# One-hot rows for eight tokens a step in two buffers, and coefficient blocks taken in pairs

## The reference

```python
    s1, i1 = lax.top_k(sc[:, :, 0], PEER_TOPK)
    s2, i2 = lax.top_k(sc[:, :, 1], PEER_TOPK)
    cand = (s1[..., :, None] + s2[..., None, :]).reshape(n_tok, PEER_HEADS, PEER_TOPK * PEER_TOPK)
    ...
    gate = jax.nn.softmax(top_s, axis=-1).astype(xn.dtype)
    ...
        hid = jax.nn.gelu(jnp.einsum('td,thkd->thk', tc, u[ec]), approximate=False)
        return jnp.einsum('thk,thkd->td', gc * hid, v[ec])
```

## Time and profile before

| | |
|---|---|
| median of 3 runs | 2471.43 us (2470.43 to 2473.3) |
| the profiled execution's own time | 2470.42 us |
| its span, first to last instruction | 2468.6 us |
| PE busy | 2433.4 us (99%) |
| DVE busy | 1891.4 us (77%) |
| ACT busy | 1256.3 us (51%) |
| granted PE clock | 1.00 |

### The profile page before, as it was taken

The page is one execution under the profiler, slowest core; times in us unless marked ns, Lnnn a source line. Parts: engine busy times, 40 slices in busy tenths (PEclk is TensorE's granted clock), DMA queues, the critical chain, the costliest instruction groups (busy, mean ns, idle before and its releaser), DMA issues.

```text
span 2468.6 us, 48181 instructions
## 1 busy us (share of the span) xinstructions
PE 2433.4 (99%) x17669; PEld 2253.8 (91%) x17669; DVE 1891.4 (77%) x3674; ACT 1256.3 (51%) x2092; POOL 132.4 (5%) x115
## 2 busy tenths in 40 slices
PE   9999999999999999999999999999999999999999
PEld 8999998999999888999988999999889999899999
DVE  6789997666666788889996666666887767887774
ACT  6755884444444434455874444444335445656343
POOL 0042000000000000052000000000000001100000
PEclk9999999999999999999999999999999999999999
DMA  7445677666665555546677666655554555634555
GB/s 241 143 158 184 191 204 249 207 214 213 210 200 188 188 187 171 189 146 201 188 219 236 213 210 207 213 196 188 187 187 144 174 183 182 142 103 156 182 182 165
DMA packets 191991, 465.16 MB, mean 188 GB/s; under 512 B 81530, under 2 KB 83706, under 8 KB 190944
## 3 DMA queue, kind: packets, MB, share of 16 engines
q1 hardware_dynamic: 118592, 419.47, 52.5%
q0 software_dynamic: 6624, 24.28, 3.3%
q10 hardware_dynamic: 66624, 19.40, 3.2%
HBM read 442.50 MB, written 20.59 MB: 188 GB/s over the span
## 4 chain that ended last, share of the span: by engine, by line
PE 49%; DVE 2%; ACT 1%; issue 0%; DMA 0%; DVEq 0%; ACTq 0%
PE acc L896 14%; PE work L550 9%; PE work L552 9%; PE work L551 9%; PE acc L550 2%; PE acc L551 1%; PE acc L552 1%; PE work L910 1%; PE work L1126 1%; DVE ring_lo L544 1%; PE work L1112 0%; PE work L1099 0%; DMA ring<-in_u 0%; ACT ring_hi L538 0%; PE work L1100 0%
## 5 line engine op out<-in xcount | busy, mean ns | idle before, releaser
L544 DVE TENSOR_TENSOR ring_lo<-ring,ring_hi 128x1024 fp32r<-128x1024 f32 (+1 forms) x757 | 918.8, 1217 | 421.0 <-ACT ring_hi L538 419.3
L538 ACT ACTIVATE ring_hi<-ring 128x1024 fp32r<-128x1024 f32 (+1 forms) x797 | 832.3, 1051 | 440.6 <-PE acc L896 359.8
L550 PE MATMUL work<-normed_hi,ring_hi 128*128 128x256 f32 (+1 forms) x2544 | 722.3, 284 | 10.2 <-DVE ring_lo L544 5.9
L551 PE MATMUL work<-normed_lo,ring_hi 128*128 128x256 f32 (+1 forms) x2544 | 713.3, 280 | 0.0
L552 PE MATMUL work<-normed_hi,ring_lo 128*128 128x256 f32 (+1 forms) x2544 | 713.3, 280 | 0.0
L896 PE MATMUL acc<-ring_hi,weighed 128*128 128x512 f32 x2048 | 587.3, 396 | 3.0 <-DVE weighed L2033 3.0
L550 PEld LDWEIGHTS work<-normed_hi,ring_hi 128*128 128x128 f32 x2544 | 478.7, 188 | 23.2 <-DVE ring_lo L544 7.1
L551 PEld LDWEIGHTS work<-normed_lo,ring_hi 128*128 128x128 f32 x2544 | 478.1, 188 | 8.3
L552 PEld LDWEIGHTS work<-normed_hi,ring_lo 128*128 128x128 f32 x2544 | 478.0, 188 | 0.0
L896 PEld LDWEIGHTS acc<-ring_hi,weighed 128*128 128x128 f32 x2048 | 372.2, 188 | 82.6 <-issue 3.2
L550 PE MATMUL work<-arena_parts,ring_hi 128*128 128x256 f32 (+1 forms) x1184 | 336.0, 284 | 2.8 <-DVE arena L2292 2.1
(11 more groups left out here) (304 smaller groups left out, 2411.2 us busy)
## 6 DMA issues: line engine op xcount, KB each, us to landing
ring<-in_u SPq DMA_DIRECT2D x256, 512.0 KB, 3.9
ring<-in_v SPq DMA_DIRECT2D x256, 512.0 KB, 4.2
ring<-in_ffn_in SPq DMA_DIRECT2D x88, 512.0 KB, 3.7
ring<-in_query SPq DMA_DIRECT2D x32, 512.0 KB, 3.8
ficients_of_later_chunks<-gate_b ACTq DMA_DIRECT2D x32, 512.0 KB, 4.9
arena<-ficients_of_later_chunks POOLq DMA_DIRECT2D x32, 512.0 KB, 4.0
ring<-in_ffn_out SPq DMA_DIRECT2D x32, 512.0 KB, 4.0
ring<-in_even_in SPq DMA_DIRECT2D x27, 512.0 KB, 4.5
```

Source lines behind the costliest of these rows:

```text
L538: act.activation(ring_hi[:, n % RING, 0:width], ring[:, n % RING, 0:width], ACT.Copy).then_inc(hi_ready, 1)
L544: eng.tensor_tensor(ring_lo[:, n % RING, 0:width], ring[:, n % RING, 0:width], ring_hi[:, n % RING, 0:width].bitcast(F32), ALU.subtract).t ...
L550: pe.matmul(out, w_hi, hi, start=start, stop=False, **more)
L551: pe.matmul(out, w_hi, lo, start=False, stop=False, **more)
```

## The change

Rows are made for eight tokens at a time (`GROUP`, a group g of two blocks; 32 groups a stage). There are two buffers of `hot_second` and of `hot_gated`, one for even and one for odd g, and two of `first`, the second one in the space of two hidden chunks that are not written until late in the stage. The instructions of DVE for 16 tokens are then seven in place of twelve: F (first), S (second), L (low part of the gated rows, all eight tokens) and H (high part of the second four tokens) for an even g, F, S and G (both parts) for an odd g. ACT still makes the high part of the first four tokens of an even g. DVE's wait for PE now stands ahead of S, for the last block of group g - 2. PE takes two blocks behind each other after every sixth step, and the last two blocks singly. ACT's list is in another order. The buffers are laid out anew in the same space.

```diff
@@ buffers @@
-        hot_first = sb("hot_first", [P, 3, 2, NKEYS, 2], F16)
...
+        pieces = desk[:, :].bitcast(F16).rearrange("p (n x) -> p n x", x=GROUP * NKEYS)
+        last_held = arena[:, (HELD - 2) * S:HELD * S].bitcast(F16)
+        hot_second = [pieces[:, n, :].rearrange("p (a e t) -> p a e t", e=NKEYS, t=2) for n in (0, 3)]
+        hot_gated = [pieces[:, n:n + 2, :].rearrange("p x (a e t) -> p x a e t", e=NKEYS, t=2) for n in (1, 4)]
+        hot_first = [v.rearrange("p (a e t) -> p a e t", e=NKEYS, t=2) for v in (pieces[:, 6, :], last_held)]
@@ PE @@
-                def coefficients(w, count):
+                def coefficients(w, c):
...
-                    b = count % 4
+                    g, b = c // 2, c // 2 % 2
...
-                    pe.wait_ge(hots_ready, count + 1)
-                    if b == 0:
-                        pe.wait_ge(act_gated, count // 4 + 1)
+                    pe.wait_ge(hots_ready, l * GROUPS + g + 1)
+                    if c % 4 == 0:
+                        pe.wait_ge(act_gated, (l * S // BLOCK + c) // 4 + 1)
...
-                            if q % 3 == 2:
+                            if q % 6 == 5 and q < K * BESIDE - 1:
+                                for c in (q // 3 - 1, q // 3):
+                                    coefficients(w0 + c, c // 4 * 4 + ORDER[c % 4])
+                            elif q >= K * BESIDE - 4 and q % 3 == 2:
                                 c = q // 3
-                                coefficients(w0 + c, built + c // 4 * 4 + ORDER[c % 4])
+                                coefficients(w0 + c, c // 4 * 4 + ORDER[c % 4])
@@ ACT @@
                 def gelu_beside(u):
                     act.wait_ge(beside_done, l * BESIDE + u + 1)
+                    if SEGMENTS[1][2] + u == HELD - 2:
+                        act.wait_ge(hots_ready, (l + 1) * GROUPS - 2)
...
                 def gate_rows(j):
                     act.wait_ge(gates_ready, l + 1)
-                    act.wait_ge(hots_used, l * (S // BLOCK) + 4 * j + 1)
+                    act.wait_ge(hots_used, l * GROUPS + 2 * j + 1)
                     if j:
-                        act.wait_ge(*done(W0[f"expert{l}.1"] + 4 * (j - 1) + ORDER.index(0)))
+                        act.wait_ge(*done(W0[f"expert{l}.1"] + 2 * (2 * j - 2) + 1))
...
-                            gate_rows(2 * p)
+                            if p == 0:
+                                gate_rows(0)
                             split_hi(act, n)
                             store(c)
                             store(c + 1)
                             gelu_beside(u)
                             store(c + 2)
+                            gate_rows(2 * p + 1)
+                            store(c + 3)
                             split_hi(act, n + 1)
-                            store(c + 3)
-                            gate_rows(2 * p + 1)
+                            gelu_beside(u + 1)
                             store(c + 4)
-                            gelu_beside(u + 1)
                             store(c + 5)
                             split_hi(act, n + 2)
-                            store(c + 6)
-                            gelu_beside(u + 2)
-                            store(c + 7)
+                            if p < PAIRS - 1:
+                                gelu_beside(u + 2)
+                                store(c + 6)
+                                gate_rows(2 * p + 2)
+                                store(c + 7)
+                            else:
+                                store(c + 6)
+                                gelu_beside(u + 2)
+                                store(c + 7)
@@ DVE @@
+                def one_hots(g, w):
...
+                    count, b, tok, final = l * GROUPS + g, g % 2, g * GROUP, g == GROUPS - 1
+                    first = hot_first[0 if final else g % 2]
+                    if g % 2 == 0 and count or final:
+                        dve.wait_ge(act_gated, (count + 1) // 2)
+                    if count >= 2:
+                        dve.wait_ge(hots_ready, count if final else count - 1)
+                    shape = [P, 4, P, 2]
...
                     dve.tensor_tensor(first, keys, row(0), ALU.is_equal).then_inc(hots_used, 1)
+                    if g >= 2:
+                        dve.wait_ge(*done(w + 2 * (g - 2) + 1))
                     dve.tensor_tensor(hot_second[b], keys, row(1), ALU.is_equal)
                     dve.wait_ge(hots_used, count + 1)
...
+                    if g % 2 == 0:
+                        high, low = [gates16[:, g, x, :].rearrange("p (a t) -> p a t", t=2).unsqueeze(2).to_broadcast(shape) for x in range(2)]
+                        dve.tensor_tensor(hot_gated[b][:, 1, :, :, :], first, low, ALU.mult)
+                        dve.tensor_tensor(hot_gated[b][:, 0, 2:4, :, :], first[:, 2:4, :, :], high[:, 2:4, :, :], ALU.mult).then_inc(hots_ready, 1)
                         return
+                    shape = [P, 2, 4, P, 2]
...
-                        for c in range(S // BLOCK):
-                            j, b = c // 4, c % 4
-                            if c % 8 in (2, 5, 7):
-                                split_lo(dve, base + c // 8 * 3 + (2, 5, 7).index(c % 8) + 1)
-                            one_hots(built + c, BLOCK * c, w0 + 4 * (j - 1) + ORDER.index(b) if j else None)
+                        for g in range(GROUPS):
+                            if g % 4:
+                                split_lo(dve, base + g // 4 * 3 + g % 4)
+                            one_hots(g, w0)
```

More of the change, by code:

```diff
@@ L139 @@
 STEP_TOKENS = 4 * BLOCK
+GROUP = 2 * BLOCK
+GROUPS = S // GROUP
 ORDER = [1, 0, 2, 3]
@@ L289, in build @@
         lead_gain = sb("lead_gain", [P, 2, K])
-        desk = sb("desk", [P, 3 * 2 * (P + 4 * HALF)])
+        desk = sb("desk", [P, 14 * 256])
         normed = desk[:, 0:K * TA].rearrange("p (k t) -> p k t", k=K)
-        product = sb("product", [P, 2, S])
+        product = desk[:, 9 * 256:11 * 256].rearrange("p (b t) -> p b t", b=2)
         sub_keys = desk[:, 0:16 * NKEYS].rearrange("p (h e) -> p h e", e=NKEYS)
[L296 to L299, removed]
-        hot_first = sb("hot_first", [P, 3, 2, NKEYS, 2], F16)
+        hot_zeros = desk[:, 11 * 256:].bitcast(F16)
         with nc.sbuf_tensor("gate_b", [P, K, S], F32) as gate_b:
@@ L420, in build @@
         val2 = view("mix", [6, 3, P])
-        val2raw = hot_first.rearrange("p b a e t -> p (b a e t)").bitcast(F32)[:, 0:2 * TA].rearrange("p (b t) -> p b t", b=2)
+        val2raw = desk[:, 11 * 256:11 * 256 + 2 * TA].rearrange("p (b t) -> p b t", b=2)
         prob2 = view("mix", [2, 3, 2, P])
@@ L898, in down @@
                     mm.then_inc(chunk_used, 1)
-                def coefficients(w, count):
-                    b = count % 4
+                def coefficients(w, c):
+                    g, b = c // 2, c // 2 % 2
                     wait_bank(pe, w)
-                    pe.wait_ge(hots_ready, count + 1)
-                    if b == 0:
-                        pe.wait_ge(act_gated, count // 4 + 1)
+                    pe.wait_ge(hots_ready, l * GROUPS + g + 1)
+                    if c % 4 == 0:
+                        pe.wait_ge(act_gated, (l * S // BLOCK + c) // 4 + 1)
                     for t in range(BLOCK):
                         for x in range(2):
-                            mm = pe.matmul(work[:, w % 4, t * P:(t + 1) * P], hot_second[b][:, t // 2, :, t % 2], hot_gated[b][:, x, t // 2, :, t % 2], start=(x == 0), stop=(x == 1))
+                            at = c % 2 * 2 + t // 2
+                            mm = pe.matmul(work[:, w % 4, t * P:(t + 1) * P], hot_second[b][:, at, :, t % 2], hot_gated[b][:, x, at, :, t % 2], start=(x == 0), stop=(x == 1))
                     mm.then_inc(bank_done[w % 4], 1)
-                built = l * S // BLOCK
                 pe.wait_ge(normed_ready, K * (l + 1))
@@ L1134, in warm @@
             def warm():
-                zeros = hot_first.rearrange("p b a e t -> p (b a e t)")
+                zeros = hot_zeros
                 pe.wait_ge(warm_ready, 1)
@@ L1371, in gate_rows @@
                     act.wait_ge(gates_ready, l + 1)
-                    act.wait_ge(hots_used, l * (S // BLOCK) + 4 * j + 1)
+                    act.wait_ge(hots_used, l * GROUPS + 2 * j + 1)
                     if j:
-                        act.wait_ge(*done(W0[f"expert{l}.1"] + 4 * (j - 1) + ORDER.index(0)))
+                        act.wait_ge(*done(W0[f"expert{l}.1"] + 2 * (2 * j - 2) + 1))
                     for t in range(BLOCK):
-                        ins = act.activation(hot_gated[0][:, 0, t // 2, :, t % 2], hot_first[:, 0, t // 2, :, t % 2], ACT.Copy, scale=act_gates[:, j, t:t + 1])
+                        ins = act.activation(hot_gated[0][:, 0, t // 2, :, t % 2], hot_first[0][:, t // 2, :, t % 2], ACT.Copy, scale=act_gates[:, j, t:t + 1])
                     ins.then_inc(act_gated, 1)
@@ L1997, in one_hots @@
```

(17 more changed lines are left out.)

5 lines of the change are left out of this document (2 added, 3 removed).

## The result

The changed kernel takes 2509.17 us, the median of 4 runs (2505.57 to 2511.55), against 2472.1 us of the kernel before (4 runs, 2470.43 to 2473.3). The ratio is 1.0149, with a 95% interval of 1.0132 to 1.0167: slower, as forecast, but by 37 us where I had 24, and outside the range of 2488 to 2504. The profiled execution took 2508.41 us, 38.0 more than the one before.

What follows compares the result with a forecast made beforehand. DVE was taken to set the pace, narrowly ahead of PE; after the change, PE's 98.9 us plus 18.25 us of waits make 117.15 against 104.9 per stage, +24.5 us over two, about 2496 us; range 2488 to 2504.

Steps and rivals of the forecast that it cites:

- The pace of the two engines: In the `upcoef` stages, per 32 tokens: DVE 13.05 us falls to 12.35, PE 12.67 falls to 12.44.
- the line through the two rows: DVE price from 512 elements (0.335 us) and 1024 (0.60), extended to G's 2048 elements: 1.13 us.
- The chain from g1 to g3: From PE's first to fourth 32-token group via ACT's late split and DVE: 8.37 us against 6.22; PE waits 2.15.
- the walk: Adding link prices through the in-order lists of PE, ACT and DVE; gave loops of 14.59 us against 13.05.
- The sum: Per stage, PE's list 98.9 us plus waits 18.25 gives 117.15 against 104.9; two stages add 24.5 us.
- rival 4: Clock halves in PE's waits, doubling its 6.22 us between g3 and g1: at most 99 us, 2595 us; chance 0.02.
- The four unseen costs: Bounds for 1024-element `is_equal`, G, a pair's second block and the four hand-overs; forecast 2492 to 2504 us.
- Rival 1: No hold-up: the high half is ready when DVE needs it; 12 us less per stage, 2460 us; chance 0.08.
- Rivals 2: A wash: the chain is about 1.5 us shorter, wait and saving cancel, 2471 us; chance 0.03.
- 3: Longer DVE instructions lose their pace: F, S, L at 1.14 us, G twice that; +36 us, 2532 us; chance 0.02.

Runs made afterwards that it cites:

- experiments 6: Changed kernel with single blocks on PE after every third step and split_hi(n + 1) ahead of the second gated rows; 2470.96 us, ratio 0.9998.
- 7: Kernel before with PE's pairs alone, old buffers and DVE instructions, split_hi(n + 1) ahead of the second gated rows; 2472.66 us, ratio 1.0006.
- (1): Changed kernel with split_hi(n + 1) moved ahead of the gated rows of g2, the next store and its spill; 2463.48 us, ratio 0.9969.
- experiment 4: Changed kernel with the spill behind store(c + 3) moved behind split_hi(n + 1); 2486.59 us, ratio 1.0061.
- experiment 3: Kernel before with split_hi(n + 1) moved behind store(c + 3), its spill and the second gated rows; 2483.86 us, ratio 1.0049.

## Why the prediction was right in the chain and wrong about the clock

**The pace of the two engines: right.** 0.60 us for 1024 elements held for `is_equal` (316.00 to 316.60), and G, which no row had shown, took 1.14 us (317.20 to 318.34) where the line through the two rows gave 1.13. The pair and its six steps are 3.09 us (I had 3.11). That PE and DVE are each close behind the other is what experiments 6 and 7 show: DVE's shorter list alone gives nothing, the pairs alone give nothing, and both together, once the split is early (1), give 8 us.

**The chain from g1 to g3: right.** 8.34 us against 8.37, eight waits in a stage, 22.8 us with the clock held up against my 24.5. Shortening it by an early split (1) or by one link (4), or making it in the kernel before (3), moved the time as the walk said, to within 3 us each.

**The clock: the step that failed.** The sum has no term for the clock: it adds the waits to PE's work at full speed. I wrote of rival 4, the clock falling in the waits, that rows speak against it and gave it 0.02. It was neither all nor nothing. I had priced only its extreme, all 16 loops at half clock for all of PE's work, 99 us, and set that against 24.5; the real case lay between, half of the waits, 1.55 us each. The evidence I put against it was one wait of 2.06 us in one execution, and a place where the clock stayed up once says little about whether it stays up 16 times. It does not even speak for that place: in the profiled execution of experiment 4 the clock fell 1.6 us behind the end of the same wait.

```profile
2256.40 0.38 PE L553 MATMUL work<-arena_parts,ring_hi 128*128 128x256 f32 x1 [2.06 <-DVE arena L2307]
```

```profile
2258.00:2261.40 3.40, 3.40 (x18) 3.40 (x18) 3.40 (x9) 1.97 (x3) 0.00 (x0) 0.53 0.61 219
```

With a term between nothing and one slow stretch for each wait (16 x 1.55 = 25 us, as a stretch turned out to cost) the range would have reached from 2488 to 2529 us. Of the changed kernel's loss 22.8 us are chain and 15.1 clock (2494.06 against 2471.29, and 2509.17 against 2494.06; their sum, 37.9, is over 37.1 because the two medians of the kernel before differ by 0.8).

**Bounds and rivals.** The four unseen costs came out inside their bounds, nearly at the values I took. Rival 1, 2460 us, is what the change gives once the hold-up is gone (2463.48 and 2461.24). Rivals 2 and 3 did not come up. One reading was off without effect: the second stretch of the earlier trace rows starts 0.47 us behind the second stage's first matmul, so that stage is 104.8 us long and not 104.4; the sum uses 104.9 for both.

## What to carry to other kernels

When two engines are as close as here (12.67 and 13.05 us for 32 tokens), shortening the list of one gives nothing that can be told, and the order of the third engine, which hands over between them, can decide: walk the chain from one pace-setting instruction to the next through every in-order list, and compare it with the pace. If such a walk shows that PE will wait regularly for a couple of microseconds, put a term for its clock beside the wait, from nothing to the cost of one slow stretch for each wait; one wait that passed without harm does not bound it. A wait that can't be removed can be cheaper with matmuls in it that nothing uses: 15 of them in each wait, and 24 in a stage's last, gave 15 us back here.

## What the runs showed of the hardware that I had not expected

The length of a wait does not settle whether the clock falls. In the profiled execution of the changed kernel 14 waits were alike (2.0 to 2.2 us); eight of them had a stretch at 1.2 GHz behind them and six did not. In the four runs the time goes with the mean granted clock: 2505.57 us at 0.994, 2508.41 at 0.993, 2509.93 at 0.992, 2511.55 at 0.991. This kernel's runs spread over 6 us and those of the kernel before over 3. In experiment 4, 14 waits of some 1.5 us had no slow stretch behind them.

In the changed kernel every slow stretch begins when PE is at work again: the first wait ended at 271.96 and the first slow stretch is 272.50 to 275.90, and the others begin 0.2 to 1.7 us behind a wait's end. That is no rule either, as the next rows show.

The Trainium skill states what may lie behind this in TensorE: Matmul & The Clock Gate (Part 1: The HAM clock gate): the clock's default is the low one and activity of PE releases it, and the hardware's watch on that activity runs freely and does not start anew with the kernel, so that the same kernel differs from run to run. The spread of the four runs agrees; that it is this that picks eight waits out of 14, no run here shows.

At the same place in the program the clock can fall or not. Late in the kernel, in code that no experiment touches, PE waits 1.45 us at the same instruction in the kernel before and in experiment 3. Before, with the clock at 1.00 around it:

```profile
2229.31 0.98 PE L1112 MATMUL work<-const,arena 128*128 128x128 f32 x5 [1.45 <-DVE arena L1806]
```

```profile
2227.00:2241.00 14.00, 10.43 (x80) 9.68 (x80) 6.04 (x14) 9.34 (x16) 0.00 (x0) 1.00 0.19 66
```

And in experiment 3, where the clock fell at 2241.6, half a microsecond before this wait ended:

```profile
2242.08 1.34 PE L1112 MATMUL work<-const,arena 128*128 128x128 f32 x5 [1.45 <-DVE arena L1806]
```

```profile
2240.00:2251.00 11.00, 9.42 (x63) 8.72 (x62) 3.05 (x9) 7.88 (x14) 0.00 (x0) 0.84 0.10 39
2241.70:2245.10 3.40, 3.02 (x15) 2.87 (x16) 0.66 (x3) 1.99 (x4) 0.00 (x0) 0.52 0.00 0
```

This one cost little, some 0.4 us: PE's next wait, 2.06 us in the kernel before, was 1.29 here, and took up most of what was lost. A slow stretch costs its 1.55 us where PE sets the pace, as in the changed stage.
